# Orders of work around the first scans, and unread products before PE's waits

## What is computed

```python
ada = silu(c) @ w_ada + b_ada          # adaLN: 9 vectors of shift, scale, gate
h = h + 0.5 * gate * swiglu(modulate(rmsnorm(h)))         # FFN 1, latent and context, D_FF = 5632
p = modulate(rmsnorm(h)) @ w_in                           # 1024 pool columns, q, k, v, z of 8 heads, beta and decay
o = gated_delta(q, k, v, g, beta)                         # 8 heads, two directions, chunks of 64 tokens
y = concat(pool_mixer(p_pool), rmsnorm(o) * silu(z))      # the pool mixer: window means, a linear per group
h = h + gate * (y @ w_out)
h = h + 0.5 * gate * swiglu(modulate(rmsnorm(h)))         # FFN 2, latent tokens only
out = rmsnorm(h)
```

## Time and profile before

| what | value |
|---|---|
| median of three runs | 2854.99 us (2853.35 to 2856.04) |
| the profiled execution | 2856.5 us, its span 2854.6 us |
| PE busy | 2799.8 us, 98% of the span |
| DVE, ACT, POOL busy | 57%, 35%, 8% |
| mean granted clock of PE | 0.994 of full |
| HBM | 211 GB/s over the span, 560 MB read |

### The profile page before, as it was taken

The page is one execution under the profiler, slowest core; times in us unless marked ns, Lnnn a source line. Parts: engine busy times, 40 slices in busy tenths (PEclk is TensorE's granted clock), DMA queues, the critical chain, the costliest instruction groups (busy, mean ns, idle before and its releaser), DMA issues. The chain is left out here.

```text
span 2854.6 us, 41614 instructions
## 1 busy us (share of the span) xinstructions
PE 2799.8 (98%) x15400; PEld 2357.2 (83%) x15400; DVE 1616.8 (57%) x2080; ACT 989.9 (35%) x1451; POOL 220.8 (8%) x373
## 2 busy tenths in 40 slices
PE   6999999999999999999999999999999999999998
PEld 4688888888888888888888888878988888888887
DVE  4567767677677752223226766745675555555444
ACT  3222222222222221111214555544354444444443
POOL 0000000000000000000101103555120000000001
PEclk9999999999999999999999999999999999999999
DMA  9866677677988956655563666685456666666664
GB/s 369 308 207 221 199 222 221 203 223 250 317 310 304 317 183 201 193 184 171 193 195 97 172 197 182 206 262 171 155 180 191 190 191 191 191 191 192 190 190 144
DMA packets 410340, 604.67 MB, mean 212 GB/s; under 512 B 52960, under 2 KB 303840, under 8 KB 401520
## 3 DMA queue, kind: packets, MB, share of 16 engines
q1 hardware_dynamic: 361824, 419.52, 47.5%
q10 hardware_dynamic: 48400, 183.63, 19.0%
HBM read 560.02 MB, written 43.02 MB: 211 GB/s over the span
## 5 line engine op out<-in xcount | busy, mean ns | idle before, releaser
L2003 DVE TENSOR_TENSOR wl<-raw,wh 128x1024 fp32r<-128x1024 f32 x638 | 784.8, 1231 | 927.2 <-ACT wh L1523 926.5
L1523 ACT CAST wh<-raw 128x1024 fp32r<-128x1024 f32 x638 | 667.7, 1048 | 1455.4 <-PE ps L785 929.9
L783 PE MATMUL ps<-x,wh 128*128 128x512 f32 (+1 forms) x2312 | 903.1, 391 | 0.1
L785 PE MATMUL ps<-x,wl 128*128 128x512 f32 (+1 forms) x2312 | 897.7, 388 | 0.0
L784 PE MATMUL ps<-x,wh 128*128 128x512 f32 (+1 forms) x2312 | 897.6, 388 | 0.0
L783 PEld LDWEIGHTS ps<-x,wh 128*128 128x128 f32 x2312 | 435.0, 188 | 96.1 <-issue 8.9
L785 PEld LDWEIGHTS ps<-x,wl 128*128 128x128 f32 x2312 | 434.7, 188 | 89.9
L784 PEld LDWEIGHTS ps<-x,wh 128*128 128x128 f32 x2312 | 435.1, 188 | 87.3
L2195 DVE SCALAR_TENSOR_TENSOR acc<-abuf,cT,acc 128x1024 f32<-128x1024 f32 x300 | 371.2, 1278 | 19.2 <-DMA abuf<-in_w_ada 18.9
L791 PE MATMUL ps<-x,wh 128*128 128x512 f32 x1408 | 349.2, 393 | 2.6 <-DVE x L2073 2.6
L791 PEld LDWEIGHTS ps<-x,wh 128*128 128x128 f32 x1408 | 254.3, 189 | 48.6 <-issue 2.9
(11 more groups left out here) (309 smaller groups left out, 2346.2 us busy)
## 6 DMA issues: line engine op xcount, KB each, us to landing
raw<-in_ffn_w_in SPq DMA_DIRECT2D x704, 256.0 KB, 3.2
raw<-in_ffn_w_out SPq DMA_DIRECT2D x176, 512.0 KB, 3.6
abuf<-in_w_ada ACTq DMA_DIRECT2D x64, 1024.0 KB, 7.1
abuf<-in_w_ada ACTq DMA_DIRECT2D x96, 512.0 KB, 3.9
x<-d_h ACTq DMA_DIRECT2D x80, 512.0 KB, 3.2
ada_t<-in_ada SPq DMA_DIRECT2D x64, 512.0 KB, 9.3
raw<-in_w_in SPq DMA_DIRECT2D x128, 256.0 KB, 3.5
raw<-in_w_out SPq DMA_DIRECT2D x32, 512.0 KB, 4.5
```

What stands on the lines that cost most here:

```text
L783: mm(out, ah, bh, start=first, stop=False, skip_group_check=reopened)
L785: return mm(out, al, bh, start=False, stop=last, skip_group_check=reopened)
L1523: nc.scalar.copy(wh[:, t % HL, :], raw[:, t % RAW, :]).then_inc(hi_done, 1)
L2003: tt(tl, raw[:, t % RAW, :], th.bitcast(F32), ALU.subtract).then_inc(lo_done, 1)
```

## The change

Seven edits:

1. SP issues UF of head 1 ahead of the first two tiles of out instead of behind them.
2. In the pool token tiles, ACT and DVE do the copies and negations of join 0 before the weight split of the same step, not after it.
3. In scan 1, DVE does fill(0) ahead of state(0), not after out_gate(0).
4. Batch 1 of the lanes is cut in five parts instead of three, and GpSimd interleaves them with place(3), cut in a part for `GI` ("g") and one for `FI` ("f"), and with out_power(1). `xl_zero` becomes `pool_wrote`, with one more use: GpSimd waits that its own copies are written.
5. PE does products that nobody reads in norm 2 (1, 4 and, behind the broadcast, 7 of 512 columns) and in norm 3 (1 and 4). They write a bank of PSUM that is not in use.
6. PE does three such products of 256 columns in the prologue, one before each of the quarters 1 to 3 of step 4.
7. The first tile of FFN 2 takes x block by block, with a wait for each.

```diff
-LANE_STEPS = (((0, 11), (11, 21), (21, BLK - 1)), ((0, 4), (4, 16), (16, BLK - 1)))
+LANE_STEPS = (((0, 11), (11, 21), (21, BLK - 1)), ((0, 4), (4, 16), (16, 22), (22, 25), (25, BLK - 1)))
...
             set_load(0)
+            level_rows(1)
             out_load(0)
             out_load(1)
-            level_rows(1)
...
+            def unread(n, out_, weights, operand):
+
+                for _ in range(n):
+                    mm(out_, weights, operand, start=True, stop=True)
+
             def norm(n, nt, bank):
 
+                def unread_norm(count):
+                    if n == 2:
+                        unread(count, ps[:, 7, :], yl[:, 0, 0:P], yh[:, 0:2, :])
+                    elif n == 3:
+                        unread(count, ps[:, 2, :], hid2(K_FF - 1, 1)[:, 0, 1, 0:P], hid2(K_FF - 2, 1)[:, 0])
...
                 i.then_inc(stat_pe, 1)
+                unread_norm(1)
                 pe.wait_ge(sq_done, squares_at(n, KT - 1))
...
                 i.then_inc(stat_pe, 1)
+                unread_norm(4)
                 pe.wait_ge(rstd_done, rms_at(n))
...
                 i.then_inc(rb_done, 1)
+                if n == 2:
+                    unread_norm(7)
...
-                if first_:
-                    pe.wait_ge(x_ready, 3 * KT + TILE_K * (k + 1))
-                i = tile_products(4 * p, range(4), t, range(TILE_K * k, TILE_K * (k + 1)), lambda kk: x2[:, kk], KT)
+                if first_ and k == 0:
+                    for kk in range(TILE_K):
+                        pe.wait_ge(x_ready, 3 * KT + kk + 1)
+                        i = tile_products(0, range(4), t, (kk,), lambda kk: x2[:, kk], KT)
+                else:
...
                         n = i * ADA_Q + q
+                        if i == 4 and q:
+                            unread(1, ps[:, 3, 0:SEQ], ident, h_lat[:, 0, :])
                         ada_quarter(q, 4 + i % 2, ada_t[:, n % ADA_RING], ada_in[n % ADA_RING],
...
             for k in range(K_TILES):
-                if k < K_TILES - AHEAD:
-                    split(0, 0, T_POOL + K_TILES + k + AHEAD)
                 if k == 2:
                     copy_y32(0)
...
                 elif k == 5:
                     negate_tn64(0)
+                if k < K_TILES - AHEAD:
+                    split(0, 0, T_POOL + K_TILES + k + AHEAD)
...
                     out_mean(h - 1)
+                    if h == 1:
+                        fill(0)
...
                     out_gate(h - 1)
-                fill(0)
+                if h != 1:
+                    fill(0)
                 fill(1)
...
+                if part == "g":
+                    i.then_inc(pool_wrote, 1)
+                    pool.wait_ge(pool_wrote, 5)
+                    return
                 if h >= 2:
-                    to_g(None, 1)
-                    to_g(1, 0)
                     pool.wait_ge(HS["pe_vn"], at("pe_vn", h - 2, 8))
...
             for h in range(1, HEADS):
-                if h + 1 < HEADS:
+                if h == 2:
+                    place(3, "g")
+                    lanes(1, 3)
+                    place(3, "f")
+                elif h + 1 < HEADS:
                     place(h + 1)
                 out_power(h - 1)
                 if h == 1:
                     lanes(1, 2)
+                elif h == 2:
+                    lanes(1, 4)
```

More of the change, by code:

```diff
@@ L411, in build @@
             sem("yp_hi"), sem("yp_lo"))
-        lt_in, xl_zero, lane_step, lanes_done, fg_out = (
-            sem("lt_in"), sem("xl_zero"), sem("lane_step"), sem("lanes_done"), sem("fg_out"))
+        lt_in, pool_wrote, lane_step, lanes_done, fg_out = (
+            sem("lt_in"), sem("pool_wrote"), sem("lane_step"), sem("lanes_done"), sem("fg_out"))
         set_in = [sem("set_in0"), sem("set_in1")]
@@ L895, in up_tile2 @@
                 pe.wait_ge(lo_done, tiles(r, UP_TILES, t) + RAW)
-                if first_:
-                    pe.wait_ge(x_ready, 3 * KT + TILE_K * (k + 1))
-                i = tile_products(4 * p, range(4), t, range(TILE_K * k, TILE_K * (k + 1)), lambda kk: x2[:, kk], KT)
+                if first_ and k == 0:
[3 more added lines that the diff above has]
+                else:
+                    if first_:
+                        pe.wait_ge(x_ready, 3 * KT + TILE_K * (k + 1))
+                    i = tile_products(4 * p, range(4), t, range(TILE_K * k, TILE_K * (k + 1)), lambda kk: x2[:, kk], KT)
                 i[-1].then_inc(tile_used, 1)
@@ L2764, in prep, with place @@
                 i.then_inc(HS["kd_set"], 1)
-            def place(h):
+            def place(h, part=None):
                 def block_to(dst, b, m):
@@ L2780, in to_g @@
                         if m is not None:
-                            block_to(GI, b, m)
+                            i = block_to(GI, b, m)
+                    return i
                 def to_f(m_even, m_odd):
@@ L2788, in to_f @@
                     i.then_inc(HS["placed"], 1)
[L2790 to L2797, removed]
+                if part != "f":
+                    pool.wait_ge(HS["level_in"], at("level_in", h, PER["level_in"]))
+                    if h:
+                        pool.wait_ge(HS["pe_tn64"], at("pe_tn64", h - 1, 1))
+                    else:
+                        pool.wait_ge(zeroed, 5)
+                        pool.wait_ge(spilled["q"], 16 * HEADS)
+                        pool.wait_ge(spilled["z"], 16 * HEADS)
+                    to_g(0, None)
+                    if h >= 2:
+                        to_g(None, 1)
+                        i = to_g(1, 0)
+                if part == "g":
+                    i.then_inc(pool_wrote, 1)
+                    pool.wait_ge(pool_wrote, 5)
+                    return
                 if h >= 2:
-                    to_g(None, 1)
-                    to_g(1, 0)
                     pool.wait_ge(HS["pe_vn"], at("pe_vn", h - 2, 8))
@@ L2820, in lanes @@
                         pool.wait_ge(fg_out, FG_DMAS * 16)
[L2821 to L2824, removed]
+                    nc.gpsimd.memset(flat, 0.0).then_inc(pool_wrote, 1)
+                    pool.wait_ge(pool_wrote, 2 * b + 1)
+                    nc.gpsimd.memset(flat[:, 0:BLK * BLK:BLK + 1], 1.0).then_inc(pool_wrote, 1)
+                    pool.wait_ge(pool_wrote, 2 * b + 2)
                 for j in range(lo, hi):
```

## The result

| | median, us | lowest to highest | runs |
|---|---|---|---|
| before | 2854.99 | 2850.26 to 2858.35 | 19 |
| changed | 2860.34 | 2856.66 to 2864.21 | 19 |

The ratio is 1.0019, 95% interval 1.0012 to 1.0025: 5.4 us slower, just under the 0.2% taken as no change, but clear of zero. The profiled execution took 2860.54 us (span 2858.7), 4.0 more than the one of before.

The account below looks back on a forecast made before the run. TensorE, busy 98% of the span, was taken as the bound. Set 3 +2.7, clock +2.5, scan 4 -0.3, prologue -2.0, norms -0.9 and -0.1 gave +1.9: median 2856.9 us, forecast's own range 2852 to 2860.5, whole range 2845 to 2863.

Parts of the forecast that it names:

- the rival of the idle unread products: Prologue and norm 2: unread products leave the clock at half; +4.8 us, 2859.8; chance 0.08.
- the stall at scan 3: Start of scan 3: late lanes delay stores, blocks and set 3; PE waits 8 to 9 us, scan starts 2.7 later.
- the prologue's 2.0: Prologue: unread products lift the clock before tile 0, limited by the weight stream; -2.0 us, range -2.8 to 0.
- the clock behind it: Scan 3, behind the stall: time lost to half clock, +2.5 us, bounds 1 and 5.2.
- scan 0, forecast 0.6 shorter: Scan 0: UF and Y sooner let scan 1 start 1.5 us sooner, the token tiles' 0.9 included.
- scan 1, for which -1.4 was forecast: Scan 1: fill(0) ahead of state(0) shortens PE's wait put down to u; 1.4 us net, bounds 1.0 and 1.6.
- that term of 2.9 for token tiles, UF and fill(0): Up to scan 2: saved waits for FI, UF and u let scan 2 start 2.9 us sooner.
- the two windows: Prologue behind tile 0: DMA below its usual 410 GB/s by 18% and 76% of 2 us; 1.9 us of transfers recoverable.
- Norm 2: Norm 2: FFN 2's first tile block by block -0.5, broadcast at full clock -0.4; sum -0.9 us, bounds -1.5 and 0.
- Norm 3: Norm 3: the same broadcast partly at full clock; -0.1 us, bounds -0.3 and 0.
- the set isn't late: Scan 3: set 3 arrives in time and all gains carry; -9.7 us, 2845.3, or 2847.1 if held at 1966.1; chance 0.20.
- a long cold stall: Scan 3: 10 us stall, half clock through the scan, no prologue gain; +7.6 us, 2862.6; chance 0.14.

Follow-up runs that it names:

- Experiment 5: Kernel before with the GpSimd edit alone (lanes of batch 1 in five parts, interleaved with place(3) and out_power(1)): 2865.02 us, ratio 1.0033.
- experiment 2: Changed kernel with the GpSimd edit undone, all other edits kept: 2853.8 us, ratio to before 0.9992.
- experiment 1: Changed kernel with SP issuing set_load(3) ahead of the lanes' stores and level_blocks(4): 2854.54 us, ratio to before 0.9997.
- 11: Kernel before with the prologue's three unread products alone: 2854.17 us, ratio 0.9993.
- 12: Kernel before with the unread products at norms 2 and 3 and FFN 2's first tile block by block: 2854.65 us, ratio 0.9996.
- 3: Kernel before with all of PE's edits alone (unread products in prologue and norms, FFN 2's first tile block by block): 2852.02 us, ratio 0.9992.
- experiment 7: Kernel before with the edits on UF, the token tiles' order and fill(0) alone: 2857.22 us, ratio 1.0003.
- 6: Kernel of experiment 1 with batch 1 of the lanes cut at 16, 25, 29: 2855.93 us, ratio to before 0.9999.
- 8: Kernel of experiment 6 with part 1 of batch 1 cut at step 13 instead of 16: 2858.15 us, ratio to before 1.0005.
- 9: Kernel of experiment 8 with SP issuing level_blocks(2) ahead of set_load(1): 2855.64 us, ratio to before 0.9999.
- 10: Kernel of experiment 6 with the lanes' stores back ahead of set_load(3): 2854.87 us, ratio to before 0.9999.
- Experiment 13: Kernel of experiment 2 with batch 1's copy of XL to XP done by ACT instead of GpSimd: 2851.54 us, ratio to before 0.9986.

## Why the prediction came out as it did

The ruling mechanism was the forecast one, and the time was in the range of the forecast, but at its very edge: the median of 2860.34 lies 0.2 under the bound of 2860.5, and 9 of the 19 runs lie above it. By the number alone the rival of the idle unread products (2859.8) was nearest; only the traces tell that it is false. The forecast of the middle, +1.9, was too low by 3.5 against the medians (+5.4), and by 2.1 against the profile (+4.0).

- *Right: the stall at scan 3.* Blocks forecast 4.5 behind the stores, seen 4.3; 12.5 from block to s_z, seen 12.8 (1961.96 to 1974.8). The wait was 9.9 (8 to 9 was said). Experiment 5 shows that the edit makes it, experiments 2 and 1 that either end of the chain removes it. The stores were forecast at 1956.7, which the prologue's 2.0 would have made 1954.7; they went at 1957.67, 3.0 later, because scan 2 began 2.9 later than forecast. From there on the steps of the chain fit: ors 3.1 into scan 2 (some 3 was said), the last lanes and XP 8.3 (8.3).
- *Right in kind, size off: the clock behind it.* Scan 3 took 1.8 longer, forecast +2.5 less 0.3.
- *Wrong: scan 0, forecast 0.6 shorter (1.5 less the token tiles' 0.9), seen 5.0 shorter.* Two things were missed. Y was to come 0.7 sooner by the scan's own start, since UF would push the tile of out and ACT's cast back; but the cast began 1.8 after the scan's start in both traces, and Y came 2.6 sooner. And the half clock that the earlier trace rows show behind the wait for UF was counted nowhere as something to gain, with no reason given. The 3.2 for UF was itself the number of one execution: the same list waited 2.2 (5), 1.4 (11), 1.0 (12) and 1.0 (3).
- *Wrong: nothing was said to be late next in scan 1*, for which -1.4 was forecast. place(2) was: 2.6 for FI, 1.6 for o, and half clock behind them, +5.3 (of which, as said, a good part also comes to kernels with the scans of before). Scan 2 began 0.7 sooner, the prologue's 1.3 taken off, where 2.9 was forecast. The failed step is that term of 2.9 for token tiles, UF and fill(0), taken as if place(2) had slack; experiment 7 measures what those edits give by themselves: nothing that can be told from 0, and its interval excludes 2.9. The token tiles' part of it held (0.9 forecast, 1.0 seen) and was given back with the rest.
- *Over by 0.7: prologue.* 2.0 forecast, 1.3 seen at head 0's join, 1.4 at the start of tile 0; since kernels that don't differ ahead of it reach the join up to 4.6 us apart (1875.3 in experiment 1, 1879.9 in 6), this size is not shown. In the forecast itself the two windows add up to 1.9, not 2.0.
- *Norm 2: right in size, not in its parts.* -1.0 was seen for -0.9. The broadcast's 0.4 can't be put down to the edit, since kernels 5, 7 and 11 have the short broadcast without it. What the sum left out is the clock of FFN 2's first tile, 4.8 us in experiment 11 and 2.8 in 12; with a start 0.9 sooner that makes 2.8, of which all but 1.0 is given back in the tiles behind it, where the next ones follow each other at 3.0 to 3.1 us instead of 2.7. That the size came out is luck. *Norm 3* -0.6 for -0.1, within what it varies by.
- The sum: scan 3 began at +4.0, where 2.7 less the prologue's 2.0 was forecast. Of these 3.3, the term of 2.9 makes 2.2, the prologue 0.7, the chain of loads 0.4. The clock took 0.4 back, the norms 0.6, and the output projection 0.1: 2.2 in all, against the 2.1 seen. The 1.4 between the profiled pair and the medians is no more than single executions differ.

Of the rivals, "the set isn't late" is refuted by the trace; "a long cold stall" had the stall of 10 us but not the price (scan 3 took 1.8 longer, not 5.2), and "the unread products do nothing" is refuted for the clock, in the prologue and at norm 2.

## What to carry to other kernels

A wait that is saved is worth what the next supplier has in slack: before counting a gain, list for each engine off the path when its next delivery would be wanted, and when it can come. Work that is moved behind a wait is late for everyone down the chain, here GpSimd's last steps, SP's stores, blocks and a set that had nothing to do with them but the queue. Where one engine's list is full between two deadlines, its order only moves the delay (experiments 6, 8, 9, 10), and what is left to try is to take work off it. Experiment 13 did that, and the wait it was meant for went; it is the only kernel here that is faster than before beyond its interval, though PE's edits are in it too. And a wait read in one trace is a sample: before pricing one, look at it in a second execution of the same list.

## What the runs showed of the hardware

- What a short wait of PE costs at the clock can be more than the wait. With 3.2 us of waiting for UF (before) scan 0 had a mean of 0.53 over 11 us. With 0.85 for ACT's Y (changed) the clock was back at full by 1910. Of kernels with one and the same list up to there, experiment 1, which waited 1.0 for Y, had a mean of 0.66 over the 10 us from 1900, and experiment 13, which waited 0.2 for Y, stayed at full:

```profile
1900.00:1910.00 10.00, 9.43 (x62) 8.16 (x61) 4.93 (x12) 3.56 (x11) 9.06 (x13) 0.66 1.08 367
1900.00:1910.00 10.00, 8.77 (x148) 7.44 (x147) 6.33 (x16) 5.35 (x14) 8.93 (x17) 1.00 1.05 389
```

- Where PE had nothing to do but wait, products that nobody reads kept the granted clock at full for the tile behind: 5.6 to 5.7 us for tile 0 of the prologue instead of 7.0 to 8.3, and 2.8 instead of 4.8 for FFN 2's first tile.
- A copy of 128 x 1024 float32 with its rows and columns exchanged took 2.07 on ACT (experiment 13) and 2.07 on GpSimd (before and changed), and 2.9 on GpSimd beside DVE's split (experiment 2).
- GpSimd's step of 0.33 (128x87) took 1.20 beside DVE's split in the changed kernel.
